# Six small tiles moved in front of the normalised input tiles, in a one-core kernel of three layers

## The reference, cut to what matters

```
def first_block(x, norm_g, ...):
    for i in range(DEPTH):                       # DEPTH = 2
        h = rms_norm(x, g[0])
        h = mlstm_mixer(...) if i % 2 == 0 else short_conv_mixer(...)
        x = x + rms_norm(h, g[1])
        h = sqrelu_mlp(rms_norm(x, g[2]), w_mlp_up[i], w_mlp_down[i])
        x = x + rms_norm(h, g[3])
...
def second_block(x, mem, ...):
    mem_n = rmsnorm(mem, mem_norm_g)
    ...
        x = x + concatenate([y_ret, y_pool]) @ w_out[l]
        x = x + cross_attn(rmsnorm(x, xa_norm_g[l]), mem_n, ...)
        x = x + conv_glu_ffn(rmsnorm(x, ffn_norm_g[l]), ...)
    return rmsnorm(x, final_norm_g)
```

## Time and profile before

| | |
|---|---|
| device time, three runs | 1009.44, 1009.82, 1010.5 us; median 1009.82 |
| profiled execution, first to last instruction | 1008.9 us, clock 0.993 of full |
| PE busy | 974.7 us, 97% |
| DVE busy | 657.2 us, 65% |
| ACT busy | 536.5 us, 53% |
| POOL busy | 191.0 us, 19% |
| bytes from HBM | 170.24 MB, 170 GB/s |

### The profile page before, as it was taken

The page is one execution under the profiler, slowest core; times in us unless marked ns, Lnnn a source line. Parts: engine busy times, 40 slices in busy tenths (PEclk is TensorE's granted clock), DMA queues, the critical chain, the costliest instruction groups (busy, mean ns, idle before and its releaser), DMA issues.

```text
span 1008.9 us, 20181 instructions
## 1 busy us (share of the span) xinstructions
PE 974.7 (97%) x8062; PEld 961.8 (95%) x8062; DVE 657.2 (65%) x843; ACT 536.5 (53%) x754; POOL 191.0 (19%) x159
## 2 busy tenths in 40 slices
PE   7999989999999899999999999989999999999996
PEld 6999989999999799989999999889999999999995
DVE  6567586665444876577665444874865779999642
ACT  5566646554443544556555444554554566666541
POOL 2021140000010400149000010455120122223101
PEclk9999999999999999999999999999999999999997
DMA  9533635555555354535555553544342545555521
GB/s 342 183 126 112 216 131 188 190 171 204 186 189 172 123 206 168 189 129 190 196 173 198 182 205 137 196 159 168 128 166 86 181 152 177 197 191 183 205 88 42
DMA packets 25844, 172.17 MB, mean 171 GB/s; under 512 B 3252, under 2 KB 3892, under 8 KB 5432
## 3 DMA queue, kind: packets, MB, share of 16 engines
q1 hardware_dynamic: 25784, 171.30, 49.0%
HBM read 170.24 MB, written 1.05 MB: 170 GB/s over the span
## 4 chain that ended last, share of the span: by engine, by line
PE 85%; DVE 7%; issue 3%; POOL 2%; ACT 2%; DMA 1%; DVEq 0%; SPq 0%; ACTq 0%; POOLq 0%
PE po L419 25%; PE po L420 25%; PE po L421 25%; DVE xnL L1252 2%; DVE wL L1245 2%; PE po L446 2%; POOL rtok L1821 2%; PE po L448 2%; PE po L447 2%; PE pn L494 1%; ACT wH L805 1%; PE pn L487 1%; PE pc L743 1%; DMA raw<-in_weights 1%; DVE diag L1271 0%
## 5 line engine op out<-in xcount | busy, mean ns | idle before, releaser
L1245 DVE TENSOR_TENSOR wL<-raw,wH 128x1024 fp32r<-128x1024 f32 x318 | 404.0, 1294 | 157.8 <-ACT wH L805 157.8
L805 ACT ACTIVATE wH<-raw 128x1024 fp32r<-128x1024 f32 x318 | 334.8, 1059 | 295.5 <-PE po L421 264.8
L419 PE MATMUL po<-xnH,wH 128*128 128x256 f32 x1376 | 396.8, 288 | 18.9 <-DVE xnL L1252 13.2
L420 PE MATMUL po<-xnL,wH 128*128 128x256 f32 x1376 | 389.9, 283 | 0.0
L421 PE MATMUL po<-xnH,wL 128*128 128x256 f32 x1376 | 389.7, 283 | 0.0
L419 PEld LDWEIGHTS po<-xnH,wH 128*128 128x128 f32 x1376 | 264.3, 192 | 23.6 <-DVE xnL L1252 9.6
L420 PEld LDWEIGHTS po<-xnL,wH 128*128 128x128 f32 x1376 | 264.5, 192 | 0.2
L421 PEld LDWEIGHTS po<-xnH,wL 128*128 128x128 f32 x1376 | 264.4, 192 | 0.0
L419 PE MATMUL po<-hH,wH 128*128 128x256 f32 x688 | 189.9, 276 | 0.0
L420 PE MATMUL po<-hL,wH 128*128 128x256 f32 x688 | 189.9, 276 | 0.0
L421 PE MATMUL po<-hH,wL 128*128 128x256 f32 x688 | 189.9, 276 | 0.0
(11 more groups left out here) (284 smaller groups left out, 1097.1 us busy)
## 6 DMA issues: line engine op xcount, KB each, us to landing
raw<-in_weights SPq DMA_DIRECT2D x158, 1024.0 KB, 4.8
x<-in_xT SPq DMA_DIRECT2D x4, 256.0 KB, 6.4
raw<-in_weights SPq DMA_DIRECT2D x2, 512.0 KB, 6.2
mem<-in_memT SPq DMA_DIRECT2D x1, 1024.0 KB, 12.6
out<-y SPq DMA_DIRECT2D x4, 256.0 KB, 2.4
decayt<-in_decay SPq DMA_DIRECT2D x1, 512.0 KB, 3.7
poolwt<-in_poolw SPq DMA_DIRECT2D x1, 256.0 KB, 3.7
par<-in_params SPq DMA_DIRECT2D x1, 164.0 KB, 3.4
```

Of the source, the lines that this page charges most:

```text
L419: pe.matmul(psum[:, n, 0:T], wH[w][:, wc], aH[:, ac, :], start=start, stop=False)
L420: pe.matmul(psum[:, n, 0:T], wH[w][:, wc], aL[:, ac, :], start=False, stop=False)
L805: act.activation(wH[b % HL][:, hs], raw[b % RAW][:, hs], ACT.Copy).then_inc(s_hi, 1)
L1245: dve.tensor_tensor(wL[b % HL][:, hs], raw[b % RAW][:, hs], wH[b % HL][:, hs].bitcast(f32), ALU.subtract)\
```

## The change

Six small tiles (`par`, `warm`, `ms`, `minus_half`, `rtok`, `rmem`) are allocated between `x` and `xnH` in place of behind `memv`. They take 1472 bytes, 1312 + 5 times 32, which is 448 past a multiple of 512. So `xnH`, `xnL`, `memH`, `memL`, `memk`, `memv`, `ident` and `ones` move 1472 bytes up and are all at offset 448; `Rs`, `Rm` and `diag` move 160 bytes up, from offset 288 to 448. `raw`, `wH`, `wL`, `x` and everything from `y` on stay where they were. No instruction, wait or loop changes; 15 blank lines at the head of the file go.

```
         x = sb("x", [P, C, T], f32)
+        par = sb("par", [P, NPAR], f32)
+        warm = sb("warm", [P, 1], f32)
+        ms = sb("ms", [P, TT], f32)
+        minus_half = sb("minus_half", [P, 2 * NH], f32)
+        rtok = sb("rtok", [P, TT], f32)
+        rmem = sb("rmem", [P, TT], f32)
         xnH = sb("xnH", [P, C, T], f32r)
         xnL = sb("xnL", [P, C, T], f32r)
         memH = sb("memH", [P, C, T], f32r)
...
         ones = sb("ones", [P, P], f32)
-        par = sb("par", [P, NPAR], f32)
         Rs = sb("Rs", [P, T], f32)
         Rm = sb("Rm", [P, T], f32)
         diag = sb("diag", [P, TT, P], f32)
-        warm = sb("warm", [P, 1], f32)
-        ms = sb("ms", [P, TT], f32)
-        minus_half = sb("minus_half", [P, 2 * NH], f32)
-        rtok = sb("rtok", [P, TT], f32)
-        rmem = sb("rmem", [P, TT], f32)
         scratch = place[0]
```

## The result

The changed kernel took 998.9, 1002.3, 993.8 and 1002.75 us, median 1000.6, against 1010.16 (1009.44 to 1012.33) for the kernel before: a ratio of 0.9892, 95% interval 0.9865 to 0.992. That is 9.6 us faster, where 22 were forecast. New is also the spread: 9 us between runs of one program that before agreed within 3.

The account below looks back on a forecast made before the run. PE was taken as the bound, busy 97% of the span with 85% of the chain. Stage savings 3.5 + 9.9 + 3.7 + 1.6 + 1.2 + 1.9 = 21.8 us gave span 987.1, time 988.0; range 983 to 1003.

Parts of the forecast that it names:

- The offset and its sign: Large products: tiles moved from offset 0 to 448 save PE 6.67 ns a matmul, 32.0 us at most; faster had 0.82.
- Rival A: Large products: the part of memory, not the offset, sets PE's pace, so no effect, 1009.8 us; chance 0.13.
- Rival D: Slabs by token: a stationary tile at 448 straddles two 512-byte blocks, adding 2.8 us, so 1012.6 us; chance 0.05.
- I take 113.3, since every long `h` stretch and three of the four `mix` stages have it: Large products: moved tiles priced at 113.3 ns a matmul in place of 120.0, 6.67 ns saved each.
- B: Moved stages fall into `out2`'s middle state, 117.8 ns: a gain of only 7.3 us, time 1002.5; chance 0.04.
- `down` and `wo` as before: Stages over tiles that don't move: the profile after would show them unchanged, forecast saving 0.
- `qk` to `up0`: `qk`, `v`, `o` were to save 3.5 us, and `f4`, `f0`, `up0` 5.0 us.
- `f6` to `f7`: `f6` to `rg` were to save 1.6 us, and `wq` with `f7` 1.2 us.
- The profile's link to the timed runs: Median of the timed runs taken as 0.9 us above the profiled span, turning 987.1 into 988.0.
- DVE as the bound of `fup`: DVE at 5.61 us a slab stops PE after some 8 slabs; `fup` and `fdown` save only 1.9 us.
- `up1` and `cin`: Steady slabs run at 5.44 us in place of 5.76; `up0` and `up1` together save 9.9 us, `cin` 3.7 us.
- nothing from the small fp32 matmuls: Matmuls over `memk` and `memv`: no gain counted, though 64 at 6.67 ns would be 0.4 us.

Follow-up runs that it names:

- e1: Kernel before with 64 unused bytes in front of `y`, so `h` and `mix` move from offset 448 to 0 like the rest: 1028.06 us, ratio 1.0169.
- e4: Kernel before with 256 unused bytes in front of `xnH`: `xn` and `mem` at 256, `h` and `mix` at 192; 1010.63 us, ratio 0.9997.
- e11: Changed kernel with the last convolution tap of `fup` cut to one column of 256, relieving DVE: 995.43 us, ratio 0.9853.
- e8: The changed kernel measured once more, unchanged, six runs: 1003.57 us (996.88 to 1008.17), ratio 0.9936.
- e2: Kernel before with small tiles moved so `xn` is at offset 64 and `mem` at 128, `h` and `mix` still at 448: 1006.0 us, ratio 0.9962.
- e9: Changed kernel plus three extra matmuls at the weights' offset once each in `up0`, `up1`, `cin`, `wo` and `fdown`: 996.73 us, ratio 0.985.
- e7: Changed kernel plus six extra matmuls at the weights' offset once each in `up0`, `up1`, `cin`, `out0` and `out1`: 999.69 us, ratio 0.9881.
- e5: Kernel before with `xn` moved to offset 96 and `mem` to 160, `h` and `mix` still at 448: 1010.9 us, ratio 1.0.
- e3: Kernel before with `xn` moved to offset 288 and `mem` to 320, `h` and `mix` still at 448: 1001.79 us, ratio 0.9909.
- e6: Unequal offsets against the kernel before: `xnH` at 64, `xnL` at 192, memory tiles at 320, `h` and `mix` at 192; 1002.95 us, ratio 0.9923.
- e12: Changed kernel with `xnL` back at offset 0, `xnH` at 448, memory tiles, `h` and `mix` at 192: 1005.21 us, ratio 0.9942.

## Why the prediction was wrong

**The offset and its sign were right.** The pace of one shape depends on where the tile lies: e1 and e4 show it, and a whole kernel at offset 0 costs 1028. Rival A is out. Rival D as well: the slabs by token went from 29.5 to 29.0 us in `v`, with the same paces as the others. The Trainium skill (SBUF — State Buffer, "SBUF: two separate sides") says that PE never waits on another engine, and its section "Specifications (TRN2)" asks for two hits or more in a 16-byte line for full rate. Neither gives a contiguous fp32 stream a second pace; the kernel before and e1 show two for `down0`, 113.3 and 120.0 ns, at offsets that are both multiples of 16. The measurement decides.

**The step that failed** is "I take 113.3, since every long `h` stretch and three of the four `mix` stages have it". The rows were read rightly and generalised wrongly. Those stretches were fast for two reasons, their offset and the stretch at 120.0 ahead of them, and the change takes the second away. The row that said so was there: `out2` at 117.8 behind a wait. I made it a rival, B, with 0.04, as if the whole kernel would be in one state or the other. Each stage draws, the ones over `h` and `mix` too, and the ten times of the changed kernel run from 993.8 to 1008.2, past B's 1003.

**The second failure is what I left out of the sum**: "`down` and `wo` as before". `down0` keeps the state that `up0` ends in, now that both lie at 448. At 16 x (5.65 - 5.44) it lost 3.4 us, more than `up0` gained. In the prediction nothing could get slower but by rival D.

**Sizes.** Of 21.8 us forecast, 12.4 came out in the profiled execution: 0.7 and 1.5 of them by luck, at the start and with the clock in `cin`; 4.2 were lost in the stages said to be untouched, and the rest (about 7.5) is short mainly in `qk` to `up0` and in `f6` to `f7`, where 117.8 or a mixture stood for 113.3. The profile's link to the timed runs was off too: in all runs that list both, the time is 2.3 to 2.5 us above the span, so the profiled execution before stood for about 1011.3, not for the median, and the forecast span of 987.1 for 989.5, not 988.0.

**Right were** DVE as the bound of `fup` (first wait after 6 slabs from slab 3 where some 8 were forecast, 5.62 us a slab, the wait at `fdown` slab 2; e11), `up1` and `cin` where they drew the fast pace, longer waits for `diag`, and nothing from the small fp32 matmuls: those over `memk` start 215 to 216 ns apart before, with `xq` alone at 448, and after, with both there. That `fup` to the end saved 2.0 us where 1.9 were forecast is in part luck: it rests on the draw. In e8's execution, with `fup` and `fdown` at 117.8, the same stretch took 994.5 - 791.9 = 202.6 us, 0.4 more than in the kernel before.

**Left open**: what at a restart decides between the states. The extra matmuls show how to leave the slow one, not why a wait leads into it. Nor do the runs say why in e2, from 64 to 448, the pace turned without a wait. Weights at other offsets weren't tried, nor extra matmuls at another offset than 0. That e9 needs 3 rather than 1 rests on one stage in which 1 failed.

## What to carry to other kernels

Where PE streams without a wait, take the distance of matmul starts per tile from windows of whole slabs, and compare it between tiles: 6% for an address is not to be seen in busy shares. If one shape shows three values, don't take the commonest for a new place, but ask what ran before each stretch. And check what a slow stretch does for its neighbours: here the stretch at 120.0 had the next one start at 113.3, which no row names. A version with a few matmuls to restore the good state (e9) was worth 1.5%, the placement alone 0.6 to 1.1% (two measurements).

## What the runs showed of the hardware

One profile each; the distance of the activation from the weights, modulo 256, and ns a matmul of 256 columns at clock 1.00 (the activation streams; in the short slabs by token, as `v`, other means between 113.3 and 120.0 occur too):

| offset | long stretches |
|---|---|
| 0 (also 256) | 120.0 only |
| 32 (tried as 288 alone) | 116.7 only |
| 64 (also 320) | 113.3 or 117.8 |
| 96 | 120.0 in the mean |
| 128 | 118.6 (`f2`, `f3`) |
| 160 | 117.4 (`f2`, `f3`) |
| 192 (also 448) | 113.3 or 117.8 |

In cycles of 2.4 GHz, three matmuls take 816, 840, 848 or 864 in the long stages, all multiples of 8, and a stretch of 30 slabs (1440 matmuls) holds one value.

Four stages (`down0`, `out1`, `down1`, `fdown`) begin on another tile without a wait, so each run shows four times what a pace does at such a joint:

| runs | ahead | behind |
|---|---|---|
| changed kernel, e7 to e11 | 448, 113.3 or 117.8 | 448, the same pace, 24 of 24 |
| before, e4, e5 | 0, 256 or 96, 120.0 | 448 or 192, 113.3, 12 of 12 |
| e3 | 288, 116.7 | 448, 113.3, 4 of 4 |
| e6 | 64 and 192, 117.8 | 192, 113.3, 4 of 4 |
| e12 | 448 and 0, 117.8 | 192, 117.8 three times, 113.3 once |
| e2 | 64, 113.3 once, 117.8 three times | 448: 117.8 behind 113.3; behind 117.8 once 113.3, twice 117.8 |

So at one distance a pace outlives a change of tile and of stage (at the starts of `wq` and `fup` too, 12 of 12). Where the distance changes, it can turn without a wait, and what stands ahead needn't be at offset 0 for 113.3 to follow. It can turn as well where the two tiles change roles: between `f4` and `f0`, `f5` and `f2`, `f6` and `f3`, where the activation goes from loaded to streaming, it went from 113.3 to 117.8 or back in 11 of 18 cases of the changed kernel and e7 to e11, without a wait. These draws are the best reading of why a program on one core spread over 11 us, 996.88 to 1008.17, in six runs; the stages' paces are known only for the profiled ones.
